# A dense layer's lower product from seven block products, placed between two upper products

## The chip, the cores and the metric

The kernel runs on one core of one Trainium2 chip. The metric is the device time of one execution in microseconds (us), lower is better. Before the change it is 9043.48 us, the median of three runs (9036.95 to 9050.25).

## The reference

A small two-layer diffusion backbone over 2048 tokens of width 1024, in float32. The even layer's feed-forward part is what the change touches; its core is

```python
def swiglu(h, w1, w3, w2):
    return (jax.nn.silu(h @ w1) * (h @ w3)) @ w2
```

with `h` 2048 x 1024, `w1` and `w3` 1024 x 2816 and `w2` 2816 x 1024. The result goes through a root-mean-square norm, a gate and a residual sum, and through a second norm that prepares the next layer. All other stages (input projection, linear attention, latent attention, Fourier mixing, the eight experts, the last norm) are the same in both kernels.

## The kernel before

The function `dense` does the attention's output projection and then the feed-forward part. The feed-forward part goes over the tokens in 4 passes of 512, and in each pass over 11 chunks of 256 hidden features: 44 chunks, numbered `n`; a pass ends at `n % 11 == 10`.

A chunk has two **upper products**, `up(2n)` (with `w1`) and `up(2n+1)` (with `w3`), and one **lower product**, `down(n)`. Each upper product is already made from seven half-size block products in place of eight (one level of a Strassen-Winograd scheme): seven block products of four matmuls each, into the PSUM banks 0 to 3. GpSimd (POOL) makes the sums of the weight blocks (`weight_sums`, four operations per upper product), VectorE (DVE) the sums of the token blocks once per pass (`token_sums`, four operations) and the sums of the results in `combine(u)`. Inside `up(u)` the order is P1, P6, P7, P2, P5, P3, P4. P2 accumulates onto P1's bank, so before it TensorE (PE) waits for `q_done`, which ScalarE (ACT) sets when `keep(u)` has copied P1 away. Before P3 it waits for `U2`, a sum that DVE makes from P6 and the kept P1.

The lower product is plain: for each of the 4 token tiles and the 2 halves of the output, two accumulating matmuls of 128 columns by 512 into one of the banks 4 to 7. DVE's `add(n)` adds each of these 8 results to `ACC` in SBUF (in a pass's last chunk into `YA`, which holds the finished rows), and PE may be at most 4 results ahead of it (`y_added`). PE's order is written out by hand: `up(2n)`, `up(2n+1)`, `down(n-1)`. DVE's order per chunk is `combine(2n)`, `combine(2n+1)`, then whatever is due of `token_sums`, `add_x(t)` and `norm_x(t)`, then `add(n-1)`.

The norms of a finished pass are spread over the chunks of the next one by `settled_beside(n, lag)`: token tile `t` has ACT's `norm_y` in one chunk, DVE's `add_x` and after it ACT's `norm_x` in the next, DVE's `norm_x` one later. So `add_x` and ACT's `norm_x` fall into the chunks with `n % 11` of 2 to 5 of the passes 2 to 4, twelve chunks; DVE's `norm_x` into 3 to 6. ACT's order per chunk is `keep(2n)`, `silu(2n)`, `keep(2n+1)`, `norm_y`, `norm_x`, and ACT's `norm_x(t)` waits for `summed`, which DVE's `add_x(t)` sets.

POOL also issues, behind each of the first 68 `weight_sums`, four DMAs that fill two scratch tensors with zeros.

Of the kernel before, what the change touches and what calls it, by code (L numbers as in the profile page):

```python
# [10 lines left out]
ALU = mybir.AluOpType  # L11
# [417 lines left out]
def dense(nc, mix_d, w_o, x0_d, gate0, cols, w1, w3, w2, gate1, x1_d, x2_d, ident_d, HX, clear):  # L429
# [12 lines left out]
    PER = TB * 2  # L442
# [4 lines left out]
    with ExitStack() as ctx:  # L447
# [6 lines left out]
        ZERO = m.sbuf("zero", [P, D])  # L454
# [11 lines left out]
        ACC = BIG[:, 0:TB]  # L466
        SM = [BIG[:, at:at + 2].rearrange("p a n -> p (a n)")[:, 0:3 * HK * P].rearrange("p (s k n) -> p s k n", s=3, k=HK) for at in (8, 4)]
        A = BIG[:, 6:8].rearrange("p b (h n) -> p b h n", h=2)
# [18 lines left out]
        s_done, a_done, y_done, y_added = (m.sem(n) for n in ("s_done", "a_done", "y_done", "y_added"))  # L487
        x1_in = [m.sem(f"x1_in{s}") for s in range(RING)]
# [116 lines left out]
        def _(pe):  # L605
# [75 lines left out]
            def down(n):  # L681
                pe.wait_ge(a_done, MULT * (n + 1))
                pe.wait_ge(w2_in[n % 2], 16 * (n // 2 + 1))
                for j in range(PER):
                    i = n * PER + j
                    if i >= 4:
                        pe.wait_ge(y_added, i - 3)
                    else:
                        pe.wait_ge(scaled0, NT)
                        pe.wait_ge(ht_a, NT)  # L690
                        pe.wait_ge(ht_v, NT)
                    t, h = j // 2, j % 2
                    for f in range(2):
                        last = nc.tensor.matmul(PS[:, 4 + i % 4], A[:, n % 2, f, t * P:(t + 1) * P], W2[:, n % 2, f, h * BANK:(h + 1) * BANK],  # L694
                                                start=f == 0, stop=f == 1)
                    last.then_inc(y_done, 1)
# [18 lines left out]
        def _(act):  # L715
# [49 lines left out]
            def norm_y(t):  # L765
                act.wait_ge(y_added, ((t // TB + 1) * FC - 1) * PER + (t % TB + 1) * 2)
# [43 lines left out]
        def _(dve):  # L810
# [45 lines left out]
            def combine(u):  # L856
                n, w = u // 2, u % 2
                T, S, H = TMP[:, w], TMP[:, 0], A[:, n % 2]
# [7 lines left out]
                def hidden(k, i, j, q, right):  # L866
                    dve.wait_ge(s_done, MULT * n + k)
                    nc.vector.tensor_tensor(H[:, i, j * HB:(j + 1) * HB], S[:, q], right, ALU.mult).then_inc(a_done, 1)
# [7 lines left out]
                if w:  # L876
                    product(P2)
                    if n >= 2:
                        dve.wait_ge(y_done, PER * (n - 1))
# [19 lines left out]

            def add(n):  # L900
                c = n % FC
                for j in range(PER):
                    i = n * PER + j
                    t, h = j // 2, j % 2
                    acc = ACC[:, t, h * BANK:(h + 1) * BANK]
                    dve.wait_ge(y_done, i + 1)
                    if c == 0:
                        nc.vector.tensor_copy(acc, PS[:, 4 + i % 4]).then_inc(y_added, 1)
                    else:
                        out = YA[:, n // FC * TB + t, h * BANK:(h + 1) * BANK] if c == FC - 1 else acc  # L910
                        nc.vector.tensor_tensor(out, PS[:, 4 + i % 4], acc, ALU.add).then_inc(y_added, 1)  # L911
# [26 lines left out]
            for n in range(N):  # L938
                combine(2 * n)
                if n == 0:  # L940
                    modulate(NT - 1)
                combine(2 * n + 1)
                if (n + 1) % FC == 0 and n + 1 < N:
                    token_sums((n + 1) // FC)
# [8 lines left out]
                if n:  # L953
                    add(n - 1)
# [9 lines left out]
        def _(pool):  # L964
# [18 lines left out]

            for u in range(2 * N):
# [2179 lines left out]
```

## Time and profile before

| | |
|---|---|
| timed runs | 9043.48 us (median of 3; 9036.95 to 9050.25) |
| profiled execution | span 9045.9 us; no time of its own stands beside the span |
| TensorE matmuls busy | 8512.0 us, 94% |
| VectorE busy | 3841.2 us, 42% |
| GpSimd busy | 2781.9 us, 31% |
| ScalarE busy | 1550.2 us, 17% |
| first upper product of `dense` | at 2084.7 us |
| last matmul of `dense` | in a row from 3761.55 us, 27.63 us long |

Busy time says which engine can be the bound; where TensorE idles, the view of waits says who ended the idle time, and the rows in order of time say what that engine had been doing.

### The profile page before, as it was taken

Reading aid. Unit: us, or ns where it says so; the run is one execution under the profiler, and the core shown is the slowest. Engines: PE = TensorE matmul, PEld = TensorE weight load, DVE = VectorE, ACT = ScalarE, POOL = GpSimd, SP = SyncE. Lnnn points to the kernel's source line nnn. Section 1 sums busy time; section 2 is a strip of 40 time slices with the busy share of each in tenths; the row PEclk is TensorE's granted clock in tenths of the full one; section 3 lists DMA queues with packets and bytes.
Section 4 is the critical chain, followed back from the end, with each engine's and each line's share of the span. In section 5 each row is a group of like instructions: output and inputs, shape, how many; then the busy total and the mean of one; then the engine's idle time right before and its main releaser. Section 6 shows DMA issues by size and latency. Waiting matters only on the chain. (4 is left out here: it accounts for less than half of the span.)

```text
span 9045.9 us, 120999 instructions
## 1 busy us (share of the span) xinstructions
PE 8512.0 (94%) x43014; PEld 6139.8 (68%) x43014; DVE 3841.2 (42%) x8373; ACT 1550.2 (17%) x3780; POOL 2781.9 (31%) x2389
## 2 busy tenths in 40 slices
PE   9975899999999999896999999999999999999994
PEld 4444566646776677544777777777777777777773
DVE  2336455433344434444444444444444334333334
ACT  1124333221010101122221222211001000000002
POOL 0011000003333433102555545544444333333333
PEclk9986999999999999997999999999999999999997
DMA  5312100045555553223455554544444333333325
GB/s 232 135 50 69 38 7 5 7 139 193 193 194 197 209 177 100 89 74 143 156 171 172 167 171 156 171 158 154 141 155 143 120 128 118 126 130 118 114 97 206
DMA packets 700618, 1203.21 MB, mean 133 GB/s; under 512 B 30321, under 2 KB 533025, under 8 KB 693366
## 3 DMA queue, kind: packets, MB, share of 16 engines
q1 hardware_dynamic: 644700, 987.05, 32.4%
q0 software_dynamic: 55584, 211.54, 6.0%
q8 instruction: 230, 3.77, 0.2%
q14 instruction: 104, 0.85, 0.0%
HBM read 959.01 MB, written 237.39 MB: 132 GB/s over the span
## 5 line engine op out<-in xcount | busy, mean ns | idle before, releaser
L2804 PE MATMUL ex_ps<-ex_w,ex_a 128*128 128x512 f32 (+2 forms) x5376 | 1654.9, 533 | 0.0
L2702 POOL TENSOR_TENSOR ex_sm<-ex_w 128x512 f32<-128x512 f32 x392 | 497.1, 1268 | 2588.6 <-PE ex_ps L2759 2555.9
L2804 PEld LDWEIGHTS ex_ps<-ex_w,ex_a 128*128 128x128 f32 (+2 forms) x5376 | 680.4, 161 | 870.2 <-issue 835.6
L2759 PE MATMUL ex_ps<-ex_xt,ex_w 128*128 x6272 | 966.2, 297 | 44.5 <-issue 42.2
L2759 PE MATMUL ex_ps<-ex_tx,ex_w 128*128 x6272 | 952.1, 295 | 23.8 <-DVE ex_tmp L2969 23.8
L2759 PEld LDWEIGHTS ex_ps<-ex_xt,ex_w 128*128 128x128 f32 x6272 | 873.1, 192 | 141.0 <-issue 141.0
L2759 PE MATMUL ex_ps<-ex_tx,ex_sm 128*128 x6272 | 891.5, 296 | 5.0 <-DVE ex_tx L2926 5.0
L2759 PEld LDWEIGHTS ex_ps<-ex_tx,ex_w 128*128 128x128 f32 x6272 | 864.0, 191 | 35.7 <-issue 20.0
L3015 DVE TENSOR_TENSOR ex_ya<-ex_ps,ex_ya 128x512 f32 x910 | 604.2, 664 | 664.5 <-PE ex_ps L2804 664.2
L2759 PEld LDWEIGHTS ex_ps<-ex_tx,ex_sm 128*128 128x128 f32 x6272 | 851.6, 193 | 5.9 <-issue 5.6
L694 PE MATMUL de_ps<-de_w,de_big 128*128 128x512 f32 x1408 | 616.4, 594 | 24.5 <-DVE de_big L911 24.5
L2708 POOL TENSOR_TENSOR ex_sm<-ex_w,ex_sm 128x512 f32<-128x512 f32 x392 | 503.2, 1284 | 30.7
L2706 POOL TENSOR_TENSOR ex_sm<-ex_w 128x512 f32<-128x512 f32 x392 | 498.0, 1271 | 30.7
L2704 POOL TENSOR_TENSOR ex_w<-ex_w 128x512 f32<-128x512 f32 x392 | 497.6, 1269 | 30.7
L694 PEld LDWEIGHTS de_ps<-de_w,de_big 128*128 128x128 f32 x1408 | 266.9, 190 | 348.7 <-issue 306.2
L976 POOL TENSOR_TENSOR de_big<-de_wr 128x512 f32<-128x512 f32 x88 | 111.3, 1265 | 1263.4 <-PE de_ps L646 1003.1
L2842 ACT ACTIVATE ex_tmp<-ex_ps 128x128 f32<-128x128 f32 (+3 forms) x392 | 116.8, 298 | 2100.5 <-PE ex_ps L2759 2099.8
L259 PE MATMUL en_psO<-en_w,en_ht 128*128 128x512 f32 (+4 forms) x1152 | 473.0, 571 | 3.6 <-ACT en_ht L301 2.0
L2759 PE MATMUL ex_ps<-ex_xt,ex_sm 128*128 x3136 | 472.5, 294 | 0.0
L2969 DVE TENSOR_TENSOR ex_tmp<-ex_ps,ex_tmp 128x128 f32<-128x128 f32 (+3 forms) x392 | 124.0, 316 | 760.8 <-PE ex_ps L2759 635.9
L2759 PEld LDWEIGHTS ex_ps<-ex_xt,ex_sm 128*128 128x128 f32 x3136 | 431.1, 191 | 0.0
L2963 DVE TENSOR_TENSOR ex_a<-ex_tmp 128x128 f32<-128x128 f32 (+3 forms) x588 | 379.6, 646 | 38.0
(403 smaller groups left out, 10618.2 us busy)
## 6 DMA issues: line engine op xcount, KB each, us to landing
ex_w<-in_o_w SPq DMA_DIRECT2D x594, 1024.0 KB, 5.0
de_wr<-in_e_w SPq DMA_DIRECT2D x88, 1024.0 KB, 5.3
xs<-de_zero POOLq DMA_DIRECT2D x136, 512.0 KB, 4.6
ys<-de_zero POOLq DMA_DIRECT2D x136, 512.0 KB, 5.4
en_ch<-in_w_mod SPq DMA_DIRECT2D x48, 1024.0 KB, 5.4
de_w<-in_e_w SPq DMA_DIRECT2D x44, 1024.0 KB, 4.9
ex_x<-xs SPq DMA_DIRECT2D x60, 512.0 KB, 5.3
proj<-en_o POOLq DMA_DIRECT2D x18, 1008.0 KB, 4.1
```

The costliest lines, as they stand in the source:

```text
L259: last = nc.tensor.matmul(psO[:, b, 0:z - a], HT[:, n % 2, k], W[:, k, a:z], start=k == 0, stop=k == KD - 1)
L694: last = nc.tensor.matmul(PS[:, 4 + i % 4], A[:, n % 2, f, t * P:(t + 1) * P], W2[:, n % 2, f, h * BANK:(h + 1) * BANK], start=f == 0, sto ...
L2702: nc.gpsimd.tensor_tensor(SM[:, w, 0], A11, A21, ALU.subtract).then_inc(sums["s3"], 1)
L2704: nc.gpsimd.tensor_tensor(A21, A21, A22, ALU.add).then_inc(sums["s1"], 1)
L2706: nc.gpsimd.tensor_tensor(SM[:, w, 1], A21, A11, ALU.subtract).then_inc(sums["s2"], 1)
L2708: nc.gpsimd.tensor_tensor(SM[:, w, 2], A12, SM[:, w, 1], ALU.subtract).then_inc(sums["s4"], 1)
L2759: last = nc.tensor.matmul(PS[:, bank, 0:h], left[:, k], right[k], start=start and k == 0, stop=k == HK - 1, skip_group_check=not start)
L2804: last = nc.tensor.matmul(PS[c * rows_n:(c + 1) * rows_n, 4 + o % 3, 0:width], A[:, b, r0:r0 + rows_n], W2[:, s, b, c0 + c * width:c0 + (c ...
L2842: nc.scalar.activation(TMP[:, w, 0, 0:h], PS[:, w, 0:h], ACT.Copy).then_inc(kept, 1)
L2963: last = nc.vector.tensor_tensor(A[:, b, c * h:(c + 1) * h], S[:, q, 0:h], right, ALU.mult)
L2969: nc.vector.tensor_tensor(slot(1), PS[:, 2, 0:h], slot(0), ALU.add).then_inc(comb["u2"], 1)
L3015: nc.vector.tensor_tensor(out, new, out, ALU.add).then_inc(y_added[t], 1)
```

## The change

The lower product is made from seven block products as well. For each pair of token tiles (`PAIRS = 2`) the 2 x 2 blocks are tile, feature half and output half; the seven products of one matmul each (128 columns by 512) go to one of the four banks as before. They are not combined per chunk: `add(n)` adds each of the 14 results to one of 14 accumulators, and in a pass's last chunk seven more operations per pair mix them into the finished rows. New are `left_sums(n)` on DVE (four sums of the hidden blocks, 256 wide, after `combine(2n+1)`) and `right_sums(n)` on POOL (four sums of the `w2` blocks, 512 wide). `A`, the hidden block, is now single. PE's order becomes `up(2n)`, `down(n-1)`, `up(2n+1)`, and DVE's `add(n-1)` stands between `combine(2n)` and `combine(2n+1)`. The tile of zeros shrinks to a quarter, and each zero DMA reads it four times.

```diff
             def down(n):
-                pe.wait_ge(a_done, MULT * (n + 1))
+                pe.wait_ge(a_sums, LSUMS * (n + 1))
                 pe.wait_ge(w2_in[n % 2], 16 * (n // 2 + 1))
...
+                pe.wait_ge(w2_sums, RSUMS * (n + 1))
+                B = [[W2[:, n % 2, f, h * BANK:(h + 1) * BANK] for h in range(2)] for f in range(2)]
+                for r in range(PAIRS):
+                    A11, A12, S1, A22 = AV[:, 0, 0, r], AV[:, 1, 0, r], AV[:, 0, 1, r], AV[:, 1, 1, r]
+                    S2, S3, S4 = (SA[:, q, r] for q in range(3))
+                    for q, (left, right) in enumerate(((A11, B[0][0]), (A12, B[1][0]), (S4, B[1][1]), (A22, WT[2]), (S1, WT[0]), (S2, WT[1]), (S3, B[0][1]))):
+                        i = n * PER + r * LOW + q
+                        if i >= 4:
+                            pe.wait_ge(y_added, i - 3)
...
+                        nc.tensor.matmul(PS[:, 4 + i % 4], left, right, start=True, stop=True).then_inc(y_done, 1)
...
             for n in range(1, N):
                 up(2 * n)
+                down(n - 1)
                 up(2 * n + 1)
-                down(n - 1)
             down(N - 1)
...
+            def left_sums(n):
+                def made(k):
+                    dve.wait_ge(a_sums, LSUMS * n + k)
+
+                dve.wait_ge(a_done, MULT * (n + 1))
+                if n:
+                    dve.wait_ge(y_done, PER * n)
+                nc.vector.tensor_tensor(SA[:, 1], AV[:, 0, 0], AV[:, 0, 1], ALU.subtract).then_inc(a_sums, 1)
+                made(1)
+                nc.vector.tensor_tensor(AV[:, 0, 1], AV[:, 0, 1], AV[:, 1, 1], ALU.add).then_inc(a_sums, 1)
+                made(2)
+                nc.vector.tensor_tensor(SA[:, 0], AV[:, 0, 1], AV[:, 0, 0], ALU.subtract).then_inc(a_sums, 1)
+                made(3)
+                nc.vector.tensor_tensor(SA[:, 2], AV[:, 1, 0], SA[:, 0], ALU.subtract).then_inc(a_sums, 1)
...
+                        if c == 0:
+                            nc.vector.tensor_copy(M[q], PS[:, 4 + i % 4]).then_inc(y_added, 1)
+                        else:
+                            nc.vector.tensor_tensor(M[q], PS[:, 4 + i % 4], M[q], ALU.add).then_inc(y_added, 1)
+                    if c == FC - 1:
...
+                        nc.vector.tensor_tensor(M6, M1, M6, ALU.add).then_inc(y_mixed, 1)
+                        nc.vector.tensor_tensor(y0[:, 0:BANK], M1, M2, ALU.add).then_inc(y_whole, 1)
+                        dve.wait_ge(y_mixed, mixed + 1)
+                        nc.vector.tensor_tensor(M7, M6, M7, ALU.add).then_inc(y_mixed, 1)
+                        dve.wait_ge(y_whole, (p * PAIRS + r) * 4 + 1)
+                        nc.vector.tensor_tensor(M1, M6, M5, ALU.add).then_inc(y_mixed, 1)
+                        dve.wait_ge(y_mixed, mixed + 3)
+                        nc.vector.tensor_tensor(y0[:, BANK:D], M1, M3, ALU.add).then_inc(y_whole, 1)
+                        nc.vector.tensor_tensor(y1[:, 0:BANK], M7, M4, ALU.subtract).then_inc(y_whole, 1)
+                        nc.vector.tensor_tensor(y1[:, BANK:D], M7, M5, ALU.add).then_inc(y_whole, 1)
...
                 combine(2 * n)
                 if n == 0:
                     modulate(NT - 1)
+                else:
+                    add(n - 1)
                 combine(2 * n + 1)
+                left_sums(n)
                 if (n + 1) % FC == 0 and n + 1 < N:
                     token_sums((n + 1) // FC)
...
-                if n:
-                    add(n - 1)
...
+            def right_sums(n):
+                pool.wait_ge(w2_in[n % 2], 16 * (n // 2 + 1))
+                if n:
+                    pool.wait_ge(y_done, PER * n)
+                B11, B12, B21, B22 = (W2[:, n % 2, f, h * BANK:(h + 1) * BANK] for f in range(2) for h in range(2))
+                nc.gpsimd.tensor_tensor(WT[0], B12, B11, ALU.subtract).then_inc(w2_sums, 1)
+                pool.wait_ge(w2_sums, RSUMS * n + 1)
+                nc.gpsimd.tensor_tensor(B12, B22, B12, ALU.subtract).then_inc(w2_sums, 1)
+                nc.gpsimd.tensor_tensor(WT[1], B22, WT[0], ALU.subtract).then_inc(w2_sums, 1)
+                pool.wait_ge(w2_sums, RSUMS * n + 3)
+                nc.gpsimd.tensor_tensor(WT[2], WT[1], B21, ALU.subtract).then_inc(w2_sums, 1)
+
             for u in range(2 * N):
                 weight_sums(u)
+                if u >= 2 and u % 2 == 0:
+                    right_sums(u // 2 - 1)
+                if u == 2 * N - 1:
+                    right_sums(N - 1)
                 for t in range(2 * u, min(2 * u + 2, n_clear)):
                     for c in clear:
-                        pool.dma_start(rows(c, t), ZERO[:, :]).then_inc(cleared, 16)
+                        pool.dma_start(rows(c, t).rearrange("p (a n) -> p a n", a=4), ZERO[:, :].rearrange("p (a n) -> p a n", a=1).to_broadcast([P, 4, D // 4])).then_inc(cleared, 16)
```

Where a tile's norms are due, VectorE has this before, from the end of one chunk's second upper product to the start of the next chunk's first (L868 is a product of hidden halves, L915 to L920 `add_x`, L924 and L926 `norm_x`, L911 `add(n-1)`, L872 the next chunk's `U2`):

```order
L895 TENSOR_TENSOR de_big<-de_big,de_ps 128x256
L868 TENSOR_TENSOR de_big<-de_big 128x256
L915 RECIPROCAL de_stat<-de_stat 128x1
L917 SCALAR_TENSOR_TENSOR hx_h<-hx_h,de_stat,de_g 128x1024
L920 TENSOR_TENSOR de_big<-de_big,hx_h 128x1024
L924 RECIPROCAL de_stat<-de_stat 128x1
L926 TENSOR_SCALAR hx_h<-de_big,de_stat 128x1024
L911 TENSOR_TENSOR de_big<-de_ps,de_big 128x512 x8
L872 TENSOR_TENSOR de_big<-de_ps,de_big 128x256
```

And the same stretch of VectorE after (lines have moved by about ten; L917 to L923 are `left_sums`, L956 to L967 the norms, L882 is `U2`):

```order
L905 TENSOR_TENSOR de_big<-de_big,de_ps 128x256
L878 TENSOR_TENSOR de_big<-de_big 128x256
L917 TENSOR_TENSOR de_sa<-de_big 128x256
L919 TENSOR_TENSOR de_big<-de_big 128x2x128
L921 TENSOR_TENSOR de_sa<-de_big 128x256
L923 TENSOR_TENSOR de_sa<-de_big,de_sa 128x256
L956 RECIPROCAL de_stat<-de_stat 128x1
L958 SCALAR_TENSOR_TENSOR hx_h<-hx_h,de_stat,de_g 128x1024
L961 TENSOR_TENSOR de_big<-de_big,hx_h 128x1024
L965 RECIPROCAL de_stat<-de_stat 128x1
L967 TENSOR_SCALAR hx_h<-de_big,de_stat 128x1024
L882 TENSOR_TENSOR de_big<-de_ps,de_big 128x256
```

Four sums came in ahead of the norms, and the eight additions went away from between the norms and `U2`.

ScalarE in such a chunk, before and after alike but for line numbers; these rows are of after, from the chunk's second `keep` (L765) over `norm_y` (L780, L782) and `norm_x` (L786, L788) to the next chunk's first `keep` and its `silu` (L770):

```order
L765 ACTIVATE de_big<-de_ps 128x256
L780 ACTIVATE de_big,de_stat<-hx_h 128x1024
L782 ACT_TABLE_LOAD
L782 ACTIVATE de_stat<-de_stat,de_eps 128x1
L786 ACTIVATE de_big,de_stat<-de_big 128x1024
L788 ACTIVATE de_stat<-de_stat,de_eps 128x1
L765 ACTIVATE de_big<-de_ps 128x256
L770 ACT_TABLE_LOAD
L770 ACTIVATE de_big<-de_ps 128x256
```

Nothing moved here: the `keep` of the next chunk's first upper product stands behind `norm_x`. What moved is TensorE's work. Before, it has between the second upper product and the next chunk's first one the lower product (L694); the rows are the last two block products of the one, the lower product, and the first four block products of the other:

```order
L646 MATMUL de_ps<-hx_h,de_big 128x256 x4
L646 MATMUL de_ps<-de_tx,de_wr 128x256 x4
L694 MATMUL de_ps<-de_w,de_big 128x512 x16
L646 MATMUL de_ps<-hx_h,de_wr 128x256 x4
L646 MATMUL de_ps<-de_tx,de_big 128x256 x4
L646 MATMUL de_ps<-hx_h,de_big 128x256 x4
L646 MATMUL de_ps<-hx_h,de_wr 128x256 x4
```

After, the same place has no lower product; it stands one upper product later, as 14 matmuls.

```order
L655 MATMUL de_ps<-hx_h,de_big 128x256 x4
L655 MATMUL de_ps<-de_tx,de_wr 128x256 x4
L655 MATMUL de_ps<-hx_h,de_wr 128x256 x4
L655 MATMUL de_ps<-de_tx,de_big 128x256 x4
L655 MATMUL de_ps<-hx_h,de_big 128x256 x4
L655 MATMUL de_ps<-hx_h,de_wr 128x256 x4
```

The first upper product of the next chunk now follows the second upper product of this one with nothing between them.

## Rows read from the trace of the kernel before

**Rows 1.** The page: busy time of each engine, share of the span, instructions.

```profile
PE 8512.0 (94%) x43014; PEld 6139.8 (68%) x43014; DVE 3841.2 (42%) x8373; ACT 1550.2 (17%) x3780; POOL 2781.9 (31%) x2389
```

**Rows 2.** Waits, 2084 to 3795 us: total us, times, longest.

```profile
PE de_ps L694 <- DVE de_big L911: 24.5, 12, 3.4
```

**Rows 3.** TensorE in order of time, a regular chunk: start, length, name.

```profile
2523.98 13.90 PE L694 MATMUL de_ps<-de_w,de_big 128*128 128x512 f32 x32
...
2537.71 1.89 PE L646 MATMUL de_ps<-hx_h,de_wr 128*128 128x256 f32 x8
...
2561.89 8.32 PE L694 MATMUL de_ps<-de_w,de_big 128*128 128x512 f32 x19
```

**Rows 4.** All engines in order of time, a chunk with norms.

```profile
2717.36 7.03 PE L694 MATMUL de_ps<-de_w,de_big 128*128 128x512 f32 x16
2717.56 0.42 DVE L895 TENSOR_TENSOR de_big<-de_big,de_ps 128x256 f32<-128x256 f32 x1 [0.84 <-PE de_ps L646]
2717.67 1.26 POOL L976 TENSOR_TENSOR de_big<-de_wr 128x512 f32<-128x512 f32 x1 [4.70 <-PE de_ps L646]
...
2718.01 1.20 DVE L868 TENSOR_TENSOR de_big<-de_big 128x256 f32<-128x256 f32 x1
...
2719.32 2.10 DVE L917 SCALAR_TENSOR_TENSOR hx_h<-hx_h,de_stat,de_g 128x1024 f32<-128x1024 f32 x1
...
2721.45 2.17 DVE L920 TENSOR_TENSOR de_big<-de_big,hx_h 128x1024 f32<-128x1024 f32 x1
...
2722.63 2.13 POOL L982 TENSOR_TENSOR de_big<-de_wr,de_big 128x512 f32<-128x512 f32 x1
...
2723.66 1.06 ACT L776 ACTIVATE de_big<-de_big 128x1024 f32<-128x1024 f32 x1 [16.08 <-DVE de_big L920]
...
2724.83 1.28 ACT L778 ACT_TABLE_LOAD   x1
2725.23 2.47 DVE L911 TENSOR_TENSOR de_big<-de_ps,de_big 128x512 f32<-128x512 f32 x4
...
2725.96 7.13 PE L694 MATMUL de_ps<-de_w,de_big 128*128 128x512 f32 x16 [1.57 <-DVE de_big L911]
2726.13 0.29 ACT L778 ACTIVATE de_stat<-de_stat,de_eps 128x1 f32<-128x1 f32 x1
...
2732.93 1.89 PE L646 MATMUL de_ps<-hx_h,de_wr 128*128 128x256 f32 x8
...
2734.86 0.38 ACT L755 ACTIVATE de_big<-de_ps 128x256 f32<-128x256 f32 x1 [8.44 <-PE de_ps L646]
```

**Rows 5.** VectorE operations with GpSimd idle, in order of time.

```profile
2716.29 0.42 DVE L868 TENSOR_TENSOR de_big<-de_big 128x256 f32<-128x256 f32 x1
...
3790.02 1.28 DVE L917 SCALAR_TENSOR_TENSOR hx_h<-hx_h,de_stat,de_g 128x1024 f32<-128x1024 f32 x1
3791.34 1.23 DVE L920 TENSOR_TENSOR de_big<-de_big,hx_h 128x1024 f32<-128x1024 f32 x1
...
3808.12 0.69 DVE L2202 TENSOR_TENSOR hx_h<-hx_h 128x512 f32<-128x512 f32 x1
```

**Rows 6.** In order of time, the end of the first pass: token sums (L849).

```profile
2481.03 7.03 PE L694 MATMUL de_ps<-de_w,de_big 128*128 128x512 f32 x16
...
2491.42 8.55 PE L694 MATMUL de_ps<-de_w,de_big 128*128 128x512 f32 x16 [3.37 <-DVE de_big L911]
...
2499.81 1.89 PE L646 MATMUL de_ps<-hx_h,de_wr 128*128 128x256 f32 x8
```

**Rows 7.** Windows there: stretch, length, busy PE, PEld, DVE, ACT, POOL, granted clock, DMA share, GB/s.

```profile
2492.00:2493.00 1.00, 1.00 (x2) 0.34 (x1) 1.00 (x2) 0.00 (x0) 0.00 (x0) 0.50 1.03 401
...
2495.00:2496.00 1.00, 1.00 (x4) 0.43 (x3) 0.55 (x1) 0.00 (x0) 0.00 (x0) 1.00 0.00 0
```

**Rows 8.** GpSimd's groups: line, operation, names, count | busy us, mean ns | idle before.

```profile
L976 POOL TENSOR_TENSOR de_big<-de_wr 128x512 f32<-128x512 f32 x88 | 111.3, 1265 | 1263.4 <-PE de_ps L646 1003.1 <-PE de_ps L614 240.5 <-PE de_ps L626 19.7
L988 POOL DMA_DIRECT2D xs<-de_zero x136 | 75.2, 553 | 4.9 <-issue 4.9
```

More of the change, by code:

```diff
@@ L453, in dense @@
         G = m.sbuf("g", [P, D])
-        ZERO = m.sbuf("zero", [P, D])
+        ZERO = m.sbuf("zero", [P, D // 4])
+        MX = m.sbuf("mx", [P, PER - 2 * TB, BANK])
+        T4 = m.sbuf("t4", [P, BANK])
+        SA = m.sbuf("sa", [P, 3, PAIRS, P])
         ident = m.sbuf("ident", [P, P])
@@ L681, in down @@
             def down(n):
-                pe.wait_ge(a_done, MULT * (n + 1))
+                pe.wait_ge(a_sums, LSUMS * (n + 1))
                 pe.wait_ge(w2_in[n % 2], 16 * (n // 2 + 1))
[L684 to L696, printed above, removed]
+                pe.wait_ge(w2_sums, RSUMS * (n + 1))
[8 more added lines that the diff above has]
+                        else:
+                            pe.wait_ge(scaled0, NT)
+                            pe.wait_ge(ht_a, NT)
+                            pe.wait_ge(ht_v, NT)
+                        nc.tensor.matmul(PS[:, 4 + i % 4], left, right, start=True, stop=True).then_inc(y_done, 1)
             turn_mix(0)
@@ L898, in combine @@
                     hidden(4, 1, 0, 2, T[:, 2])
-            def add(n):
[L901 to L911, printed above, removed]
+            def left_sums(n):
[3 more added lines that the diff above has]
+                if n:
+                    dve.wait_ge(y_done, PER * n)
+                nc.vector.tensor_tensor(SA[:, 1], AV[:, 0, 0], AV[:, 0, 1], ALU.subtract).then_inc(a_sums, 1)
[5 more added lines that the diff above has]
+                nc.vector.tensor_tensor(SA[:, 2], AV[:, 1, 0], SA[:, 0], ALU.subtract).then_inc(a_sums, 1)
@@ new lines, in add @@
+            def add(n):
+                c, p = n % FC, n // FC
+                if c == 0 and p:
+                    dve.wait_ge(y_whole, 4 * PAIRS * p)
+                for r in range(PAIRS):
+                    M = [ACC[r * LOW + q] for q in range(LOW)]
+                    for q in range(LOW):
+                        i = n * PER + r * LOW + q
+                        dve.wait_ge(y_done, i + 1)
+                        if c == 0:
[3 more added lines that the diff above has]
+                    if c == FC - 1:
+                        M1, M2, M3, M4, M5, M6, M7 = M
+                        y0, y1 = (YA[:, p * TB + 2 * r + t] for t in range(2))
+                        mixed = (p * PAIRS + r) * 3
+                        dve.wait_ge(y_added, n * PER + (r + 1) * LOW)
+                        nc.vector.tensor_tensor(M6, M1, M6, ALU.add).then_inc(y_mixed, 1)
[8 more added lines that the diff above has]
+                        nc.vector.tensor_tensor(y1[:, BANK:D], M7, M5, ALU.add).then_inc(y_whole, 1)
```

22 lines of the change are left out of this document (14 added, 8 removed).

## The prediction

> **What bounds the kernel now.** I began with the page: TensorE's matmuls fill 94% of the span and no other engine half of it [rows 1], so only what TensorE computes or waits for in this stage can count. The rows of a regular chunk give its price. From one lower product's start to the next are 2561.89 - 2523.98 = 37.91 us; the lower product takes 2537.71 - 2523.98 = 13.73 us, the fourteen block products of the two upper ones 24.18, or 1.727 each [rows 3]. 44 such chunks are 1668 us, and from the first upper product to the end of the last lower one are 1704 us, so the stage is TensorE's own work plus some 36 us of waits. Two kinds of wait are to be seen. At the end of a pass the lower product takes 2499.81 - 2481.03 = 18.78 us, 5.05 too long: 3.37 idle, because DVE adds nothing while it makes the token sums, and the rest at half the clock (0.50 granted in the first window, 1.00 later) [rows 6, 7]. In a chunk with both `add_x` and DVE's `norm_x` it takes 2732.93 - 2717.36 = 15.57 us, 1.84 too long [rows 4]. The waits for these additions are 24.5 us in twelve places, which is 3 of 3.37 and 9 of 1.57 [rows 2]: three ends of a pass, and three chunks in each of three passes. In all 3 x 5.05 + 9 x 1.84 = 31.7 us of waiting; the rest is the start.
>
> **What is saved.** 14 matmuls of the same shape stand where 16 stood: 13.73 x 2/16 = 1.72 us per chunk, 75.5 us in 44. PE no longer meets DVE's norms and token sums in the lower product, so the 31.7 us go too. Together -107.2 us.
>
> **What the additions cost.** A lower result now comes every 0.858 us. Four additions in a row took 2.47 us, 0.62 each, and a lone one 0.69, read from PSUM [rows 4]; they keep pace, four banks deep, and cost nothing in 40 chunks. POOL's four `right_sums` are as large as the `weight_sums`, 1.27 us each alone [rows 8]: 5.1 us in the first half of `up(2n+1)`, needed 24 us later. POOL then has 15.2 us of sums in 36.2; hidden. The zero DMAs have four pieces per row where they had one. Issuing one took 0.553 us [rows 8]; no row shows one of 512 pieces, so the bounds are 0.55 and four times that, 2.2. Eight per chunk are 4.4 to 17.7 us, with the sums 20 to 33 us of 36.2. I cost it at nothing; the cover is gone at (36.2 - 15.2) / 8 = 2.6 us each. The Trainium skill ("DMA: Bandwidth & Descriptors", "Anatomy of one DMA") says one can emit many descriptors before the added cost shows, which is nearer the lower bound; no run here shows it.
>
> **The new wait.** Call T the end of `up(2n+1)`. Before, the 13.7 us of `down(n-1)` came next, and DVE's and ACT's tail lay under it. After, `up(2n+2)` follows at once, and its P2, the fourth block product, wants `q_done` by T + 3 x 1.727 = T + 5.2. That flag is set by ACT's `keep(2n+2)`, behind ACT's `norm_x(t)`, which waits for DVE's `add_x(t)`, which now stands behind `left_sums`. So in the twelve chunks with `add_x`:
> - DVE's last subtraction ends at T + 0.62, and the last hidden product takes 1.20 instead of 0.42, because POOL's `weight_sums` began at T + 0.31: it ends at T + 1.86 [rows 4, 5]. In these rows a DVE operation with two inputs in SBUF and a POOL operation take turns: L917 takes 2.10 beside POOL and 1.28 alone, L920 2.17 and 1.23, POOL's own 2.13 and 1.27 [rows 4, 5, 8].
> - The four left sums are of the form of L868, 0.42 alone, 1.20 beside POOL. POOL has three operations left, so three of the four wait one out: 3 x (1.10 + 0.42) + 0.45 is about 4.7, to T + 6.6.
> - POOL is then done with its sums. Reciprocal 0.2, L917 1.28, L920 1.23: T + 9.35.
> - ACT: square, 1.18 until the root can start, 0.29 for it, 0.38 for `keep`: T + 11.3. In the chunk with `n % 11 == 5` there is no `norm_y` ahead, and a table load of 1.28 comes in between, as at 2724.83 [rows 4]: T + 12.6.
> - PE stands for 6.1 us, nine times, and 7.4, three times. 3.37 us of idleness were enough to halve the clock, for 5.05 - 3.37 = 1.7 us of loss [rows 6, 7]; I add 1.7 each time. 9 x 7.8 + 3 x 9.1 = 97.5 us.
>
> Bounds: with no turns taken (0.42 each) the left sums end at T + 2.9, the stands are 2.4 and 3.7 us and may not cost the clock, 33 us; with L917 and L920 also beside POOL, 1.7 us more each, 118 us. I take the middle, since L868 in just this place took 1.20.
>
> The Trainium skill ("SBUF — State Buffer", "Who interferes with whom") has the rule that a VectorE instruction with two SBUF inputs and a GpSimd one that reads SBUF lock each other out, the later one blocking fully. By it the sum is the 97.5; by the lone price of L868 it would be the 33. This trace is on the rule's side (1.20 against 0.42).
>
> **Token sums.** At the end of three passes they stand behind the left sums, and `up(2n+2)` now wants them at its second block product, T + 1.73. From T + 6.6 four of 1024 at 1.23 and the gaps end at T + 11.7: 9.9 us of standing and 1.7 of clock, 3 x 11.6 = 34.8 us. With no turns it is 3 x 7.9 = 24.
>
> **Mixing.** Seven operations of 512, two SBUF inputs, 0.69 each [rows 5], some 4.8 us per pair, four banks ahead. The first pair's additions end 6.9 us into the lower product; mixing lasts until 11.8, so the fifth result of the second pair starts at 12.5 instead of 9.4: 3.1 us. The second pair's mixing runs under the next upper product beside `right_sums`, and `U2` comes some 1.4 us late for P3. 4.5 us in three passes, 13.5. At the very end nothing hides them: left sums before the last lower product 3.0 (POOL idle), 3.1 as above, and the last mixing 4.8, 10.9 us.
>
> **Sum.** 97.5 + 34.8 + 13.5 + 10.9 = 156.7 against 107.2: +49.5 us. On the profiled span of 9045.9 that is 9095; the median of the runs lies 2.4 us under the span, so I say **9093 us**, 0.54% slower. A measurement of this kernel can tell about 0.2%, 18 us, from no change.
>
> **Rivals.**
> - *The left sums do not wait for POOL* (ends on the other side). For it: when DVE's small operations follow each other within 0.05 us they may keep the port. Against it: L868 waited in every such chunk I read. The place is T + 0.7 to T + 6.6. The new waits become 33 + 24 + 9.3 + 10.9 = 77, the net -30, 9013 us. It decides at 4.0 us per `add_x` chunk on average in place of 8.1: faster if `q_done` comes before about T + 8.
> - *ACT's `keep` never holds PE*, so that the change does what it seems to: 107.2 - 59.2 = 48 us are left, 8995 us. Only if I misread ACT's order, which the rows of the order show.
> - *The lower product doesn't get shorter*: DVE paces it. An addition of 0.69 with 0.2 of signalling is 0.89 against 0.858; if they don't overlap, 14 x 0.03 x 44 = 18 to 25 us more, 9115. Against it: 2.47 for four.
> - *Dearer turns and clock*: norms beside POOL too, clock lost longer or in the mixing: up to 35 us more, 9130.
> - *POOL becomes the bound through the zero DMAs*: at 3 us each, 15.2 + 24 against 36.2, 3.0 us x 33 chunks, 9192.
>
> **How the numbers follow.** Forecast 0.66 (its own range 9065 to 9120), left sums free 0.12, never held 0.04, paced 0.07, dearer 0.07, POOL 0.04. The range takes in the forecast, the paced and the dearer case and part of the way to the first rival: 9050 to 9135. Faster by over 0.2% (under 9025): the first two rivals, less a little, 0.14. Slower (over 9062): 0.76. Between: 0.10.
>
> **What the profile after would show.** Waits of PE on ACT's `keep` line (L765), twelve of 6 to 7.5 us; three on `token_sums` of about 10; granted clock 0.50 behind them; a regular chunk of 36.2 us; lower products of 12.0; left sums of 1.2 us, except the last ones; no wait of PE on POOL. I would be wrong if the left sums took 0.42 each beside POOL, if PE's waits stayed under 4 us, or if POOL's DMA issues grew beyond 2.6 us.

## The result and the profile after

The changed kernel took 9083.6 us, the median of four runs (9080.39 to 9089.61). The kernel before took 9044.8 on the same chip, the median of four (9036.95 to 9050.25). The ratio is 1.0047, with a 95% interval of 1.0033 to 1.0062: slower by about half a per cent, as forecast (9093), within the range.

The page of the changed kernel's profile has less matmul time than before [rows 1] and more of everything that VectorE and GpSimd do, in a span of 9079.4 us:

```profile
PE 8462.9 (93%) x42838; PEld 6120.7 (67%) x42838; DVE 4233.3 (47%) x8869; ACT 1547.0 (17%) x3780; POOL 3037.3 (33%) x2565
```

A regular chunk in TensorE's rows, in order of time (start, length, name):

```profile
2543.11 1.89 PE L655 MATMUL de_ps<-hx_h,de_wr 128*128 128x256 f32 x8
...
2567.28 1.88 PE L706 MATMUL de_ps<-de_w,de_big 128*128 128x512 f32 x4
...
2579.30 1.03 PE L655 MATMUL de_ps<-hx_h,de_wr 128*128 128x256 f32 x4
```

The lower product takes 2579.30 - 2567.28 = 12.02 us where it took 13.73, and the chunk 36.19 where it took 37.91 [rows 3]. That is the gain that the change is made for, 75.5 us in 44 chunks. The waits of TensorE in the stage, 2080 to 3860 us (total us, times, longest), show the price; before there was one group of 24.5 us there besides the start [rows 2]:

```profile
PE de_ps L655 <- ACT de_big L765: 72.0, 12, 7.0
PE de_ps L655 <- issue: 28.6, 3, 9.5
PE de_ps L706 <- DVE de_big L937: 9.6, 4, 2.4
PE de_ps L706 <- DVE de_sa L923: 2.8, 1, 2.8
```

L765 is ScalarE's `keep`, the three waits under "issue" are those for the token sums, L937 is the additions behind a mixing, L923 the last left sums. The first group is the forecast's main term. One of its twelve in order of time, all engines (compare [rows 4]); the second upper product ended at T = 2681.04:

```profile
2681.24 0.42 DVE L905 TENSOR_TENSOR de_big<-de_big,de_ps 128x256 f32<-128x256 f32 x1 [0.84 <-PE de_ps L655]
2681.35 1.27 POOL L1018 TENSOR_TENSOR de_big<-de_wr 128x512 f32<-128x512 f32 x1 [4.01 <-PE de_ps L655]
...
2682.70 1.33 POOL L1020 TENSOR_TENSOR de_wr<-de_wr 128x512 f32<-128x512 f32 x1
...
2682.94 1.37 DVE L917 TENSOR_TENSOR de_sa<-de_big 128x256 f32<-128x256 f32 x1
2684.11 1.33 POOL L1022 TENSOR_TENSOR de_big<-de_wr 128x512 f32<-128x512 f32 x1
...
2684.34 1.37 DVE L919 TENSOR_TENSOR de_big<-de_big 128x256 f32<-128x256 f32 x1
...
2686.78 0.72 POOL L1046 DMA_DIRECT2D xs<-de_zero  x1
2687.16 0.42 DVE L923 TENSOR_TENSOR de_sa<-de_big,de_sa 128x256 f32<-128x256 f32 x1
...
2687.69 1.29 DVE L958 SCALAR_TENSOR_TENSOR hx_h<-hx_h,de_stat,de_g 128x1024 f32<-128x1024 f32 x1
...
2689.01 1.23 DVE L961 TENSOR_TENSOR de_big<-de_big,hx_h 128x1024 f32<-128x1024 f32 x1
...
2690.27 1.06 ACT L786 ACTIVATE de_big<-de_big 128x1024 f32<-128x1024 f32 x1 [16.37 <-DVE de_big L961]
...
2691.65 0.36 ACT L765 ACTIVATE de_big<-de_ps 128x256 f32<-128x256 f32 x1
2692.07 3.78 PE L655 MATMUL de_ps<-hx_h,de_wr 128*128 128x256 f32 x8 [5.69 <-ACT de_big L765]
2695.64 2.53 PE L655 MATMUL de_ps<-de_tx,de_wr 128*128 128x256 f32 x8
```

Read it downwards: three left sums, each 1.37 us beside GpSimd, the fourth 0.42 when GpSimd has gone over to issuing DMAs; then the two operations of `add_x`; then ScalarE's square and root; then the `keep` for which TensorE stands. The first block product behind the stand takes 3.57 us in place of 1.73, at a granted clock of 0.50 (stretch, its length, busy PE, PEld, DVE, ACT, POOL, clock, DMA share, GB/s):

```profile
2692.00:2693.00 1.00, 0.93 (x2) 0.84 (x3) 0.78 (x2) 0.40 (x2) 0.00 (x0) 0.50 1.02 348
...
2698.00:2699.00 1.00, 1.00 (x6) 0.88 (x5) 0.76 (x2) 0.00 (x0) 0.00 (x0) 1.00 0.99 401
```

For the ledger I took the length of every upper and lower product, start to start, less its undisturbed length of 12.09 and 12.02 us (13.73 for the lower product before); and for the whole **stage** the time from the first upper product (L655) to the first operation of the Fourier stage (a memset on VectorE). The stage is 3807.24 - 2084.69 = 1722.6 us before and 3860.41 - 2072.15 = 1788.3 us after, 65.7 longer. The stage's length is what the experiments below are compared by, next to their times.

### The profile page after: what moved, and what is told of

It is laid out like the page before. It is cut to its first block and busy times, and to the rows that moved or that the text cites. A ratio compares the mean times of both kernels' runs of the same rounds, so it can differ in the third digit from the quotient of the medians.

```text
span 9079.4 us, 121463 instructions
## 1 busy us (share of the span) xinstructions
PE 8462.9 (93%) x42838; PEld 6120.7 (67%) x42838; DVE 4233.3 (47%) x8869; ACT 1547.0 (17%) x3780; POOL 3037.3 (33%) x2565
## 5 line engine op out<-in xcount | busy, mean ns | idle before, releaser
L2862 PE MATMUL ex_ps<-ex_w,ex_a 128*128 128x512 f32 (+2 forms) x5376 | 1654.9, 533 | 0.0
L655 PE MATMUL de_ps<-hx_h,de_wr 128*128 128x256 f32 x1408 | 355.0, 398 | 72.0 <-ACT de_big L765 72.0
L3021 DVE TENSOR_TENSOR ex_a<-ex_tmp 128x128 f32<-128x128 f32 (+3 forms) x588 | 380.3, 647 | 37.5
L259 PEld LDWEIGHTS en_psO<-en_w,en_ht 128*128 128x128 f32 x1152 | 217.7, 194 | 240.6 <-issue 236.8
L1403 DVE COPY ma_pt<-ma_ps 128x512 f32<-128x512 f32 (+1 forms) x320 | 197.7, 636 | 376.9 <-PE ma_ps L1303 375.4
```

The lines of the kernel that those rows point to most:

```text
L259: last = nc.tensor.matmul(psO[:, b, 0:z - a], HT[:, n % 2, k], W[:, k, a:z], start=k == 0, stop=k == KD - 1)
L655: last = nc.tensor.matmul(PS[:, at, 0:HB], left[:, k], right[:, k], start=start and k == 0, stop=k == HK - 1, skip_group_check=not start)
L1403: nc.vector.tensor_copy(PT[:, p % 2, a:z, u % 2], ps[:, 5 + (u * NG + j) % 2, 0:(z - a) * P].rearrange("p (k n) -> p k n", n=P)).then_inc( ...
L2862: last = nc.tensor.matmul(PS[c * rows_n:(c + 1) * rows_n, 4 + o % 3, 0:width], A[:, b, r0:r0 + rows_n], W2[:, s, b, c0 + c * width:c0 + (c ...
L3021: last = nc.vector.tensor_tensor(A[:, b, c * h:(c + 1) * h], S[:, q, 0:h], right, ALU.mult)
```

## The experiments

The kernel before and the changed kernel once more, each run once and profiled, to see what repeats.

**b_again**, the kernel before. 

> The kernel before, unchanged, profiled a second time. The two profiles showed the stage of the change 65.7 us longer, but the rest of the kernel 32 us shorter, though nothing was changed there (12.5 us of it before the stage begins). If that is chance from one execution to the next, this profile has the feed-forward stage at 1722 us again (within 3), and the parts ahead of it and behind it at other values than 2084.7 and 5238.7 us, moved by 10 us or more towards those of the changed kernel. If it belongs to the changed program, they come out within 3 us of 2084.7 and 5238.7.

It took 9032.84 us, and its stage 3797.71 - 2072.27 = 1725.4 us, 2.9 more than in the first profile: the idle times are the same (24.5 us in twelve), but the lower product at the third pass's end takes 20.07 us in place of 17.36, with the same 3.4 us of standing in it. So a stage of before is known to some 3 us. **a_again**, the changed kernel. 

> The changed kernel, unchanged, profiled a second time, for the same question. By chance: stage 1788 us within 3, the part ahead of it away from 2072.2 us and the part behind it away from 5219 us by 5 us or more. If it belongs to the program: both within 3 us.

It took 9091.49 us, its stage 1788.4, and its waits are the same to the tenth: 72.0 in twelve, 28.6 in three. What doesn't repeat is when the dense stage begins: the last operation on the PSUM tile of the stage ahead of it (a copy on ScalarE) started at 1811.0 and 1798.5 us in the two profiles of before, and at 1798.4 and 1809.9 in the two of after. Such a difference of 12 us between two profiles is chance, not the change. Another difference does repeat, and I come to it last.

**x_act** takes the link out of the chain that the forecast says all of it hangs on: ScalarE's order.

```diff
                 if n:
                     keep(2 * n)
+                    t = settled_beside(n - 1, 1)
+                    if t is not None:
+                        norm_x(t)
                 silu(2 * n)
...
-                t = settled_beside(n, 1)
-                if t is not None:
-                    norm_x(t)
```

> The changed kernel with ScalarE's normalization of the third half row (norm_x) moved behind keep(2n+2), so that the copy of the first product of the next pass pair no longer queues behind a normalization that queues behind the sums. Theory of the prediction (the twelve stands of TensorE are this one wait, passed on through ScalarE's queue): the twelve waits for keep, 72.0 us in all, are gone, and with them the cold clock behind them (31.7 us in the changed kernel); what is left is the next thing that VectorE is late with behind its sums, the first quarter sum U2 of that pair: about 1.9 us nine times and 1.0 us three times, none of which stops TensorE for long, so the stage is about 80 us shorter than in the changed kernel, near 1708 us, and the kernel near 9003 us. Rival (VectorE itself is late, whoever hands its sums on): TensorE stands as long at U2, and the stage stays within 20 us of 1788 us.

It took 9005.4 us (8998.39 to 9013.8), 0.9958 (95% interval 0.9941 to 0.9974) of the kernel before, and its stage 1702.1 us. Its waits in the stage, besides those at the ends of the passes, which stay:

```profile
PE de_ps L655 <- DVE de_big L882: 19.2, 15, 1.7
```

(Three of the fifteen stood there already, behind a mixing.) There is none for `keep`. The stand of 5.69 us has become one of 1.65 for `U2`, which VectorE makes late, and such an upper product takes 14.0 us where it took 20.4 to 20.9. VectorE does the same work in the same order in both kernels; TensorE stood because its fourth block product hung on an engine queued behind VectorE. 86.2 us of the stage, more than the change adds to it, hang on the order of two steps on an engine that is 17% busy.

**x_port** takes the turns away: GpSimd begins its sums for a chunk's second upper product only when TensorE has made three block products of the first. In the changed kernel it begins them at T, beside the left sums.

```diff
                 if u >= 2:
-                    pool.wait_ge(prod_done, PROD * (u - 1))
+                    pool.wait_ge(prod_done, PROD * (u - 1) + (3 if w else 0))
```

> The changed kernel, but GpSimd begins the second weight sums of a chunk only when the next upper product has done three of its block products (T + 5.2), not at T. If the left sums are slow because they take turns with GpSimd, they now take 0.42 to 0.45 us each instead of 1.36, end near T + 2.9 instead of T + 6.5, and the twelve waits of TensorE on ScalarE's keep fall from 72 us in all to about 27 (1.9 to 2.1 nine times, 3.2 three times) with no loss of clock behind most of them; the three waits for token sums fall from 9.5 to about 6 us. Stage 1788 to about 1710 us, the kernel faster than the changed one by 70 to 85 us. The rival, that the place of the lower product alone makes the wait and the turns are small, has the left sums unchanged or the waits down by less than 1 us each, and gains under 15 us.

It took 9020.67 us (9014.41 to 9026.62), 0.9976 (0.9966 to 0.9986) of the kernel before, and its stage 1719.6 us. The groups of VectorE's first three left sums in the changed kernel (x44: busy us, mean ns), and the same in x_port:

```profile
L917 DVE TENSOR_TENSOR de_sa<-de_big 128x256 f32<-128x256 f32 x44 | 59.9, 1362 | 1.5
L919 DVE TENSOR_TENSOR de_big<-de_big 128x256 f32<-128x256 f32 x44 | 59.4, 1351 | 1.5
```

```profile
L917 DVE TENSOR_TENSOR de_sa<-de_big 128x256 f32<-128x256 f32 x44 | 18.7, 425 | 1.5
L919 DVE TENSOR_TENSOR de_big<-de_big 128x256 f32<-128x256 f32 x44 | 18.7, 425 | 1.5
```

And x_port's waits in the stage:

```profile
PE de_ps L655 <- ACT de_big L765: 28.6, 12, 3.3
PE de_ps L655 <- issue: 17.8, 3, 5.9
PE de_ps L706 <- DVE de_big L937: 12.6, 4, 5.3
```

The same instruction on the same data, 1362 ns with a GpSimd sum running and 425 without. The waits for `keep` fall from 5.69 and 6.9 us to 2.06 and 3.35, near the forecast's lower bound of 2.4 and 3.7. With the turns gone the stage is 68.7 us shorter. One place got worse: at the first pass's end a DMA issue held GpSimd back (idle 3.65 us for nothing that the profile shows), its delayed sums then ran beside the first pair's mixing, and three mixing operations took 1.49 to 1.75 us in place of 0.69, hence the 5.3.

**x_dve** leaves the turns and changes VectorE's order: the norms of a settled tile go ahead of the second half's `combine` and the left sums.

```diff
                     add(n - 1)
+                if n == FC:
+                    dve.wait_ge(g1_in, 16)
+                t = settled_beside(n, 1)
+                if t is not None:
+                    add_x(t)
+                t = settled_beside(n, 2)
+                if t is not None:
+                    norm_x(t)
                 combine(2 * n + 1)
                 left_sums(n)
                 if (n + 1) % FC == 0 and n + 1 < N:
                     token_sums((n + 1) // FC)
-                if n == FC:
...
-                    norm_x(t)
```

> The changed kernel, but VectorE does the settled tiles' add_x and norm_x between add(n-1) and combine(2n+1), beside the second upper product, where it has some 7 us free. Theory: ScalarE's norm_x is then done long before the next chunk's keep, so the twelve waits on keep (72 us idle and 32 us of half clock) go wholly, and since the norms there run beside right_sums they cost VectorE about 5 us in a slack of 7: U2 still comes in time. Stage 1788 to about 1685 us, 100 us faster than the changed kernel, waits for token sums unchanged at 9.5. A rival has VectorE too late for U2 there (norms and GpSimd's right sums in turns): waits of 1 to 3 us on line L882 in nine chunks, a gain of 60 to 80 us.

It took 8981.14 us (8980.54 to 8987.3), 0.9934 (0.9917 to 0.995) of the kernel before, and its stage 1681.5 us. The norms now start behind the last lower addition, under the second upper product:

```profile
2618.64 0.69 DVE L937 TENSOR_TENSOR de_mx<-de_ps,de_mx 128x512 f32<-128x512 f32 x1 [0.17 <-PE de_ps L706]
...
2619.44 1.66 DVE L958 SCALAR_TENSOR_TENSOR hx_h<-hx_h,de_stat,de_g 128x1024 f32<-128x1024 f32 x1
2620.10 2.13 POOL L1033 TENSOR_TENSOR de_w<-de_w 128x512 f32<-128x512 f32 x1
...
2621.14 2.18 DVE L961 TENSOR_TENSOR de_big<-de_big,hx_h 128x1024 f32<-128x1024 f32 x1
...
2623.43 1.58 DVE L967 TENSOR_SCALAR hx_h<-de_big,de_stat 128x1024 f32<-128x1024 f32 x1
...
2624.93 0.41 DVE L882 TENSOR_TENSOR de_big<-de_ps,de_big 128x256 f32<-128x256 f32 x1
```

They pay for GpSimd's right sums beside them (2.18 us where L961 took 1.23), and it costs nothing: `U2` (L882) is made before the sixth block product asks for it. No wait for L765 or L882 is left in these chunks; 106.8 us of the stage are gone, the 103.7 that the twelve chunks had cost and 3 more. The new placement had opened room for VectorE here, under the second upper product, and the change had left the norms behind it.

**x_tok** makes the token sums ahead of the left sums, and TensorE's waits for them one by one.

```diff
                 combine(2 * n + 1)
-                left_sums(n)
                 if (n + 1) % FC == 0 and n + 1 < N:
                     token_sums((n + 1) // FC)
+                left_sums(n)
...
                 if u % (2 * FC) == 0:
-                    pe.wait_ge(t_made, 4 * (p + 1))
+                    pe.wait_ge(t_made, 4 * p + 2)
```

(with two more waits, for 3 and 4 of them, ahead of the third and the last block product.)

> The changed kernel with VectorE's four token sums of a new pass made ahead of the left sums in place of behind them, and TensorE's waits for them given out one by one (the second, third and fourth sum each where its product needs it). The changed kernel stood 9.5 us at each of its three passes' ends. Theory (the stand is the four left sums of 1.4 us, 4.5 us in all with the wait for their neighbour's turn, plus the four token sums): the three stands fall from 9.5 to about 4.9 us each, the three pass ends take back about 14 us, the stage is near 1774 us and the kernel near 9070 us. Rival (the stand's length is set by what came before it, the last rows of the lower product, or the left sums pushed back make the lower product wait instead): the stand stays within 1.5 us of 9.5, or its gain comes back as a wait of the lower product for left sums, and the stage stays at 1788 us.

It took 9066.22 us (9057.46 to 9075.4), 1.0024 (1.0014 to 1.0034) of the kernel before, and its stage 1768.0 us, 20.3 shorter. Its waits for `keep` and for the token sums:

```profile
PE de_ps L655 <- ACT de_big L769: 72.0, 12, 7.0
PE de_ps L655 <- issue: 13.4, 3, 4.5
```

The stands are 4.5 us where 4.9 was expected, and the gain is 20.3 us where 14 was: the upper product with such a stand takes 18.49 us where it took 24.5 to 24.6, so a shorter stand also lost 1 us less by the clock, and the twelve upper products with `norm_x` are 2 us shorter in sum, though their idle times stay as they were, to the tenth.

**x_old** keeps the seven products and the mixing, and goes back to the old placement.

```diff
                 up(2 * n)
-                down(n - 1)
                 up(2 * n + 1)
+                down(n - 1)
```

(the gated values have two buffers for it; VectorE makes `add(n - 1)` and the left sums last, GpSimd the right sums one upper product later.)

> The same seven products for eight and the same mixing, but placed as before: both upper products of the next pair first, the lower product behind them (the gated values in two buffers, left sums behind VectorE's additions, right sums one product later). It shows what the placement between the upper products is worth against the seven products alone. By the prediction's terms: the products save 75.5 us; the mixing costs 16 us and the end 13.6 us as placed in the changed kernel; VectorE's additions of the last pairs fall due while only four banks (3.4 us of TensorE's work) cover them, so that the nine row ends with both kinds of normalization stand about 7.2 us each, the three others with an addition 5 us, three with a normalization alone 1.6 us, and the three passes' ends 9 us: about 100 us of stands, with the clock's loss behind them. The stage is then about 1759 us, 30 us shorter than in the changed kernel and 36 us longer than before the change. Rival (the placement is what covers VectorE's work, and without it TensorE also waits for the left sums at every lower product): waits of the lower product for left sums of 3 us or more in each of 22 pairs, and a stage of 1820 us or more.

It took 9065.79 us (9060.23 to 9077.07), 1.0025 (1.0015 to 1.0034) of the kernel before, and its stage 1773.3 us: 15.0 less than with the new placement, 14 more than expected. Its waits from 2080 to 3800 us, and TensorE's rows in a chunk with norms:

```profile
PE de_ps L707 <- DVE de_big L940: 84.4, 21, 6.8
PE de_ps L655 <- DVE de_big L883: 7.1, 3, 2.7
```

```profile
2632.30 2.08 PE L707 MATMUL de_ps<-de_big 128*128 128x512 f32 x2 [5.00 <-DVE de_big L940]
2634.17 1.91 PE L707 MATMUL de_ps<-de_big,de_sa 128*128 128x512 f32 x2
2635.87 1.91 PE L707 MATMUL de_ps<-de_w,de_sa 128*128 128x512 f32 x2
2637.58 2.20 PE L707 MATMUL de_ps<-de_w,de_big 128*128 128x512 f32 x4
2639.62 1.02 PE L707 MATMUL de_ps<-de_w,de_sa 128*128 128x512 f32 x2
```

Nine lower products take 20.2 us, 8.1 to 8.2 too long, where 7.2 was expected: 5.00 idle and some 3.1 of clock. That is 8 us of the miss; most of the rest is at the very end, some 17 us where 13.6 was put, at the mixing, and in the three chunks with an addition alone. The rival's waits for left sums in every chunk don't exist; there is one, of 5.9 us, ahead of the last lower product. So the seven products alone bring no gain in either placement, and the new one is the dearer by 15 us as long as VectorE's norms and ScalarE's `norm_x` keep their old places.

**x_all** has the edits of x_dve, x_port and x_tok together.

> The three edits that took something back, together: VectorE's additions and normalizations of a settled pair stand ahead of the second half's combining and the left sums (as in x_dve), SBUF's sums on GpSimd wait until TensorE's third product has been made where the left sums run (as in x_port), and the token sums come ahead of the left sums (as in x_tok). Theory (the three act on different waits, so they add): no wait for keep, three token stands of about 4 us in place of 9.5, left sums of 0.42 us in place of 1.36 us; the stage near 1656 us against 1681.5 us with x_dve alone, and the kernel 8955 us, ratio to the kernel before 0.990. Rival (once the additions stand ahead, nothing waits for the left sums and their turns with GpSimd cost nothing, and the token sums meet the lower product instead): the same as x_dve within 10 us, 8981 us.

It took 8953.0 us (8947.75 to 8960.2), 0.99 (0.9883 to 0.9916) of the kernel before, and its stage 1654.9 us, 133.4 less than in the changed kernel. Its waits:

```profile
PE de_ps L710 <- DVE de_big L941: 12.6, 4, 5.4
PE de_ps L655 <- issue: 5.1, 3, 1.7
PE de_ps L710 <- DVE de_sa L927: 2.8, 1, 2.8
PE de_ps L655 <- DVE de_big L886: 2.0, 3, 0.7
```

No long wait is left but the first pass's mixing, for the reason seen in x_port. The edits do more than add up at the tokens: the three stands are 1.7 us where x_tok alone had 4.5, since GpSimd's sums no longer run beside the token sums. The group of the first token sum, in x_tok and in x_all (x3: busy us, mean ns):

```profile
L863 DVE TENSOR_TENSOR de_tx<-hx_h 128x1024 f32<-128x1024 f32 x3 | 6.8, 2280 | 0.0
```

```profile
L863 DVE TENSOR_TENSOR de_tx<-hx_h 128x1024 f32<-128x1024 f32 x3 | 3.7, 1219 | 0.0
```

The sum checks: 1722.6 - 75.5 - 29.1 (the waits of before) + 5.8 (tokens) + 18.0 (mixing) + 13.6 (end) is 1655.4.

**The experts' stage.** In the eight profiles of kernels with the seven products the experts' stage, whose code is the same, took 4669 to 4672 us, and 4687.4 and 4685.3 in the two profiles of before (from TensorE's first instruction on the stage's PSUM tile to the start of VectorE's last addition from it; in b_again 8916.1 - 4230.8, in a_again 8974.8 - 4302.9). The waits there, first b_again, then a_again:

```profile
PE ex_ps L2759 <- issue: 40.7, 14, 3.9
```

```profile
PE ex_ps L2817 <- issue: 30.9, 10, 4.0
```

TensorE stands there for nothing that the profile shows, 14 times before and 10 times with the change, 9.8 us less in all. **a_pad658** and **a_pad329** move the code in TensorE's program and nothing else:

```diff
             down(N - 1)
+            for _ in range(1316):
+                pe.wait_ge(prod_done, 1)
```

(two such waits make one instruction; 658 in place of 1316 for a_pad329.)

> The changed kernel with 658 instructions on TensorE that only wait for a semaphore that has long been reached, behind the last lower product, where TensorE stands 30 us anyway. The change took 704 matrix instructions (88 products of four passes, each a weight load and a multiply) out of TensorE's program and put 46 waits in, so this puts the code behind the dense stage back where it stood in TensorE's program. The question is the stage of the experts, whose code the change doesn't touch and which took 4685 to 4687 us in the kernel before and 4670 to 4672 us in all those with the seven products. Theory (the experts' stage pays for where its code lies in TensorE's program: with the kernel before, TensorE stood 14 times with nothing waited for, 3 to 4 us each, 40.7 us in all, with the changed one 10 times, 30.9 us): 13 to 15 such stands and 4685 us for that stage. Rival (it comes from elsewhere, such as another engine's program or the memory's layout): 10 stands and 4672 us. The dense stage stays at 1788 us.

> The same with half as many, 329, instructions that only wait. Theory (the place of the code in TensorE's program decides): the number of long stands and the time of the experts' stage may lie at either of the two values or between them, from 4670 to 4687 us, and should not leave that range by more than 5 us. Rival (the place doesn't matter): 10 stands and 4672 us, as with 658.

They took 9137.43 and 9109.94 us, one run each; the 658 idle instructions cost some 48 us behind the lower product (TensorE's gap there is 78.34 us in place of 30.39) and the 329 some 12, which has nothing to do with the question. The count of 704 in the expectation isn't what the profile shows: its pages have 43014 - 42838 = 176 matmuls and as many weight loads fewer, 352 instructions, so that the 329, not the 658, come near to what was taken out. The experts' stages took 4678.8 us (9020.0 - 4341.2) and 4676.3 (8993.0 - 4316.7). The waits, a_pad658 first:

```profile
PE ex_ps L2819 <- issue: 36.0, 15, 3.9
```

```profile
PE ex_ps L2819 <- issue: 35.7, 14, 3.9
```

For a_pad658 neither the theory nor the rival came true; a_pad329 stayed within its wide theory and missed the rival. The stage is 7 and 4 us longer than the longest of those eight profiles, and the number of stands went back from 10 to 15 and 14: idle instructions put into TensorE's program ahead of the stage do change it, as far as one profile of each can show. But the time did not come back to 4685. In b_again eleven of the stands are of 2.3 to 3.9 us; in the padded kernels eight are of 3.1 to 3.9, as in the changed kernel, and the added ones are of 1.0 to 1.6 us. What makes the three long ones is open.

## Why the prediction was right, point by point

The forecast was 9093, and 9083.6 came; the main reason it gave is the one that the runs bear out, though the nearness of the two numbers is in part luck. By its steps, predicted first, then read from the profile after:

- *Products saved*: 75.5; 12.02 against 13.73 us per chunk, so 75.5.
- *Waits gone*: 31.7; the ledger of before gives 29.1, because two of the three token stands cost 3.6 and not 5.05 (17.36 us for the lower product against the 18.78 that I had read at the first). In b_again the three cost 5.2, 3.6 and 6.3, behind the same 3.37 us of idleness.
- *Additions and GpSimd's sums hidden*: yes; a regular chunk is TensorE's own 36.19 us, and TensorE waits for no GpSimd sum. The zero DMAs rose from 0.553 us to issue one [rows 8] to 0.82 on average for `xs` and 0.91 for `ys`; but these overlap, and from the start of one to the start of the next are 0.64 us where there were 0.54, four in a row taking 2.95 in place of 2.17. Both are far below the 2.6 at which they would have been seen. The rule of the Trainium skill ("DMA: Bandwidth & Descriptors", "Anatomy of one DMA"), that many descriptors come before an added cost shows, held in the main: four times as many pieces took GpSimd 1.2 to 1.4 times as long, not four.
- *The new wait*: twelve, through VectorE's left sums, `add_x`, ScalarE's `norm_x` and `keep`. The left sums' end was put at T + 6.6 and came at T + 6.54; `keep`'s at T + 11.3, and TensorE went on at T + 11.03. The first hit has a slip in it: 3 x (1.10 + 0.42) + 0.45 is 5.0 and not 4.7, so that the working gives T + 6.9 and stands 0.3 us longer. In the rows the left sums start 1.40 us apart beside GpSimd, not 1.52. The stands: 6.1 and 7.4 predicted, 5.69 and 6.9 measured, 72.0 us in place of 77. x_act showed that they go through ScalarE, x_port that the turns make three fifths of their length (72.0 us against 28.6).
- *The clock*: put at 1.7 us for each stand, from one stand of 3.37. It was 2.6 in the mean: the twelve upper products are 103.7 us too long in all, 31.7 beyond the stands. This is the term that was mis-sized most, 97.5 against 103.7 in sum, with the stands' own 5 us going the other way.
- *Token sums*: 34.8; 37.5 measured (12.4 to 12.5 each, 9.53 of it idle).
- *Mixing*: 13.5; 15.9. The second pair's wait was 2.4 us and not 3.1, since the seven operations follow each other 0.6 to 0.7 us apart and end after 4.35 us, not 4.8; but the clock took 2.0 us more with it, and the upper product behind is 0.94 longer.
- *The end*: 10.9; 13.6. The lower product behind the 2.81 us of standing began at a granted clock of 0.50 (its first four matmul rows took 3.2 us in place of 1.7), which I had not counted.

In the stage these come to -75.5 - 29.1 + 103.7 + 37.5 + 15.9 + 13.6 = +66.1, and the profiles say +65.7 (+63.0 in the second pair). The forecast said +49.5. The medians differ by 38.8 us, with an interval of some 30 to 56. Of what brought this below the forecast, not above it, the runs show one part that repeats, the experts' stage, 13 to 15 us shorter with unchanged code. The rest is within what changes from run to run: in the first pair of profiles the part ahead of the stage was 12.5 us shorter after, in the second pair 11.5 longer. So the nearness of 9083.6 to 9093 is partly luck: the dense stage was 16 us dearer than forecast, for which the clock behind the twelve stands alone has 11, and a stage that nobody touched gave nearly as much back.

Of the rivals, the left sums do wait for their turn (1.36 us in the mean, 0.42 without GpSimd); x_port is that rival built, and with 0.9976 it comes out on the side that the rival named. That `keep` never holds TensorE is what x_act builds: 9005.4 against the 8995 of that rival. VectorE did not pace the lower product: no regular one took more than 12.02 us. The rule in the Trainium skill ("SBUF — State Buffer", "Who interferes with whom"), by which the later of two such instructions is blocked fully, fits VectorE's side of the trace: L917 starts at 2682.94, the GpSimd sum beside it ends at 2684.03, and L917 only at 2684.31. It is not the plain sum of the two: 1.09 us of remainder and 0.42 would be 1.51, and 1.37 was measured; GpSimd's own sums took 1.33 us where one alone takes 1.27.

## What to carry to other kernels

When work is moved from between two stretches of TensorE, list what lay under it on the other engines: here 13.7 us of lower product had covered VectorE's norms, and the eighth that was saved was worth less than that cover. Follow a needed flag through every queue that it passes; moving a normalization of the nearly idle ScalarE behind one copy was worth 86 us, and the norms ahead of the left sums 107 (either by itself, for both remove the same twelve stands), on a change that by itself lost 66. And price a stand at its length and the clock behind it.

## What the runs showed of the hardware that was not expected

- What a stand costs beyond itself isn't regular, and doesn't simply grow with it. Beyond the idle time a product was longer by 0.3 us behind 1.65 of idleness (x_act, every time); behind 2.06 by 0.3 in six cases and 1.95 in three of the same kernel (x_port); behind 2.4 by 0.3 or 2.0; behind 3.37 by 0.3, by 1.7 to 1.8, or by 3.0 (the two profiles of before); behind 5.69 by 2.65 to 3.15, but behind 6.96 by 1.9, every time (after); behind 9.53 by 2.9 to 3.0 (after), and by 1.7 to 3.3 in x_act; and by 3.0 to 3.2 behind 5.00 in x_old's lower product, where only matmuls of 512 columns follow.
- Of four zero DMAs in a row the profile gives 0.72, 0.83, 0.92 and 1.03 us, each one more than the last, though they start 0.64 us apart: the durations overlap, so their sum is not GpSimd's time. Before the change the four were 0.72, 0.54, 0.53 and 0.53 us, one behind the other.
- Taking instructions out of TensorE's program in one stage went with a later stage of unchanged code being shorter by 13 to 18 us in 4685, and putting idle ones in made it longer by 4 and 7. Why is open.
